# Conditioning groups of a 1-core model kernel closed one by one, and its tiles placed anew over the layers

## The reference

```python
def first_block(x, ...):            # DEPTH = 2: attention, then mLSTM
    h = x
    for i in range(DEPTH):
        if i % 2 == 0: h = h + dilated_attention_mixer(rms_norm(h, attn_norm[i // 2]), ...)
        else:          h = h + mlstm_mixer(rms_norm(h, mlstm_norm[i // 2]), ...)
        h = h + swiglu(rms_norm(h, ffn_norm[i]), ffn_w_in[i], ffn_w_out[i])
    return rms_norm(h, final_norm)

def second_block(x, c, ctx, ...):   # layers: neighbourhood attention, conformer, short conv, neighbourhood attention
    for i in range(4):
        mod_l = (silu(c) @ mod_w[i] + mod_b[i]).reshape(b, 6, 1, 1024)
        mod_c = (silu(c_ctx) @ mod_w[i] + mod_b[i]).reshape(1, 6, 1, 1024)
        a = rmsnorm(x, norm1_g[i]) * (1 + mod_l[:, 1]) + mod_l[:, 0]
        x = x + mod_l[:, 2] * mixer_i(a, ...)
        m = rmsnorm(x, norm2_g[i]) * (1 + mod_l[:, 4]) + mod_l[:, 3]
        x = x + mod_l[:, 5] * (square(relu(m @ mlp_w1[i])) @ mlp_w2[i])
        # the same for ctx with mod_c, while a later attention still needs it
    return rmsnorm(x, final_g)
```

## Time and profile before

| | |
|---|---|
| time, median of 3 runs | 3109.58 us (3107.96 to 3117.44) |
| the profiled execution's own time | 3106.95 us |
| its span in the profile | 3104.8 us |
| PE busy | 2923.8 us |
| DVE busy | 2011.8 us |
| ACT busy | 1186.5 us |
| POOL busy | 357.5 us |
| DMA | 451.79 MB, mean 146 GB/s |

### The profile page before, as it was taken

One profiled execution on the slowest core, in us unless ns is written; L12 is line 12 of the kernel. 1 busy time (PEld: TensorE's weight loads), 2 busy tenths in 40 slices (PEclk: granted clock), 3 DMA queues, 4 the chain that ended last, 5 costly groups with the idle time before them and its releaser, 6 DMA issues.

```text
span 3104.8 us, 41474 instructions
## 1 busy us (share of the span) xinstructions
PE 2923.8 (94%) x17130; PEld 2499.0 (80%) x17130; DVE 2011.8 (65%) x3228; ACT 1186.5 (38%) x1927; POOL 357.5 (12%) x539
## 2 busy tenths in 40 slices
PE   7998999889989989999999899999999999998898
PEld 7998899879977767888865578887877888777898
DVE  6776777767765667666653576666767664444665
ACT  5443443544443443332231442223224222343544
POOL 0000101000013221000123100001010000143000
PEclk9999999989989999999999999999999999999999
DMA  6544566436646543444445334443443442366353
GB/s 223 166 167 143 171 230 225 138 125 227 232 156 136 106 72 103 151 142 150 147 135 149 104 129 142 154 145 128 143 143 122 148 151 95 85 106 95 123 182 131
DMA packets 362269, 451.79 MB, mean 146 GB/s; under 512 B 12656, under 2 KB 332432, under 8 KB 362080
## 3 DMA queue, kind: packets, MB, share of 16 engines
q1 hardware_dynamic: 326976, 329.89, 32.5%
q0 software_dynamic: 34944, 118.65, 15.2%
q10 hardware_dynamic: 160, 0.59, 0.1%
HBM read 438.67 MB, written 1.05 MB: 142 GB/s over the span
## 4 chain that ended last, share of the span: by engine, by line
PE 79%; DVE 11%; ACT 5%; issue 3%; DMA 2%; POOL 1%; SPq 0%; DVEq 0%; ACTq 0%; POOLq 0%
PE ps L1025 23%; PE ps L1027 23%; PE ps L1026 23%; DVE MX L1551 2%; DVE lo L1497 2%; PE ps L1194 2%; DVE lo L1500 2%; ACT hi L1226 1%; PE ps L1181 1%; PE ps L1046 1%; PE ps L1048 1%; PE ps L1047 1%; DMA NB<-in_na_rpb 1%; PE ps L1090 1%; DVE NB L1509 1%
## 5 line engine op out<-in xcount | busy, mean ns | idle before, releaser
L1025 PE MATMUL ps<-XN,hi 128*128 128x256 f32 (+1 forms) x3008 | 1023.2, 340 | 79.0 <-DVE XN L1523 31.8
L1026 PE MATMUL ps<-XN,hi 128*128 128x256 f32 (+1 forms) x3008 | 1009.4, 336 | 0.0
L1027 PE MATMUL ps<-XN,lo 128*128 128x256 f32 (+1 forms) x3008 | 1008.4, 335 | 0.0
L1025 PEld LDWEIGHTS ps<-XN,hi 128*128 128x128 f32 x3008 | 584.9, 194 | 165.0 <-DVE XN L1523 39.1
L1027 PEld LDWEIGHTS ps<-XN,lo 128*128 128x128 f32 x3008 | 584.6, 194 | 54.8
L1026 PEld LDWEIGHTS ps<-XN,hi 128*128 128x128 f32 x3008 | 585.4, 195 | 52.8
L1497 DVE TENSOR_TENSOR lo<-raw,hi 128x1024 fp32r<-128x1024 f32 (+1 forms) x313 | 385.3, 1231 | 290.1 <-ACT hi L1226 287.8
L1551 DVE CUSTOM_DVE_ANT_0 MX<-MW,C 128x1024 bf16<-128x1024 f32 x384 | 485.5, 1264 | 40.4 <-DMA MW<-in_mod_w 33.8
L1226 ACT ACTIVATE hi<-raw 128x1024 fp32r<-128x1024 f32 (+1 forms) x313 | 326.2, 1042 | 439.9 <-PE ps L1027 436.0
L1500 DVE TENSOR_TENSOR lo<-raw,hi 128x1024 fp32r<-128x1024 f32 (+1 forms) x313 | 381.6, 1219 | 0.0
L1027 PE MATMUL ps<-H,lo 128*128 128x512 f32 (+1 forms) x1024 | 371.2, 363 | 0.0
(11 more groups left out here) (225 smaller groups left out, 3417.4 us busy)
## 6 DMA issues: line engine op xcount, KB each, us to landing
raw<-in_mlp_w SPq DMA_DIRECT2D x128, 1024.0 KB, 5.0
MW<-in_mod_w POOLq DMA_DIRECT2D x192, 512.0 KB, 3.8
raw<-in_ffn_w_in SPq DMA_DIRECT2D x44, 1024.0 KB, 5.0
raw<-in_attn_w_in SPq DMA_DIRECT2D x36, 1024.0 KB, 4.9
raw<-in_na_wqkv SPq DMA_DIRECT2D x24, 1024.0 KB, 4.9
raw<-in_ffn_w_out SPq DMA_DIRECT2D x16, 1024.0 KB, 5.0
raw<-in_mlstm_w_in SPq DMA_DIRECT2D x12, 1024.0 KB, 5.0
raw<-in_cv_w SPq DMA_DIRECT2D x12, 1024.0 KB, 6.3
```

What stands on the lines that cost most here:

```text
L1025: e.matmul(out, whi, xhi, start=first, stop=False)
L1026: e.matmul(out, whi, xlo, start=False, stop=False)
L1027: i = e.matmul(out, wlo, xhi, start=False, stop=last)
```

## The change

- A layer's groups close one by one: `mod_close` runs after tiles 15, 23, 39 and 47 of a layer, each over its own groups; `("mod", layer, group)` and `("gs", layer, which)` are separate names, and each norm and residual waits for its own. `conditions_for(layer, group)` asks for the tiles up to that group only, and now stands before residuals too.
- `beside` adds half the pace, and is called after each tile of a unit, not in the first unit after a norm (`outer`) and not in the last unit before one (`quiet`).
- Paces: none in attention and mLSTM, 0.65 in SwiGLU, 0.25 in neighbourhood attention, 1.15 from the first MLP to the third, 0.5 in the last MLP.
- The loads of C and of the first MW stand after the first unit of attention instead of ahead of all.

```diff
@@ -246,6 +246,9 @@
 
+CLOSING = {15: (0, 2, 0), 23: (2, 3, None), 39: (3, 5, 1), 47: (5, 6, None)}
+
+
@@ -332,17 +335,17 @@
             self.do("mod_load", n + 1)
-        if n % 48 == 47:
-            self.do("mod_close", n // 48)
+        if n % 48 in CLOSING:
+            self.do("mod_close", n // 48, *CLOSING[n % 48])
 
     def beside(self):
-        self.credit = min(self.credit + self.pace, 2.0)
+        self.credit = min(self.credit + self.pace / 2, 2.0)
         if self.credit >= 1:
...
 
-    def conditions_for(self, layer):
-        while self.parts < (layer + 1) * 48:
+    def conditions_for(self, layer, i):
+        while self.parts < layer * 48 + (i + 1) * 8:
             self.condition()
@@ -350,7 +353,7 @@
 
-    def linear(self, w, layer, k0, kt, c0, cols, x, evac, adv=1, outer=False, until=None):
+    def linear(self, w, layer, k0, kt, c0, cols, x, evac, adv=1, outer=False, until=None, quiet=False):
 
@@ -370,7 +373,7 @@
                 evac(t, *banks[i])
-            if group[-1] == tiles[-1] // 2 or outer:
+            if not (outer or quiet):
                 self.beside()
@@ -387,7 +390,7 @@
             evac(t, b, u)
-            if t == ntt // 2 - 1:
+            if t % (ntt // 2) == ntt // 2 - 1:
                 self.beside()
@@ -422,7 +425,7 @@
         if shift is not None:
-            self.conditions_for(shift[0])
+            self.conditions_for(shift[0], shift[1] + 1)
         s = self.rstd(n)
@@ -436,6 +439,8 @@
     def residual(self, j, n, gate, b, u, last):
+        if gate is not None:
+            self.conditions_for(*gate)
         self.do("residual", self.norms, j, n, gate, b, u, last)
@@ -455,7 +460,7 @@
             self.linear(w, layer, 0, KT, c * 256, 256, x, evac, adv=adv if first else 1, outer=bool(first),
-                        until=first)
+                        until=first, quiet=c == 3)
             if first:
@@ -483,6 +488,10 @@
 
+    def begin_conditions():
+        p.do("conditions")
+        p.do("mod_load", 0)
+
@@ -495,7 +504,7 @@
                 if first:
-                    p.pend.append(lambda: p.do("conditions"))
+                    p.pend.append(begin_conditions)
                 p.pend.append(rotate)
@@ -534,7 +543,7 @@
                     p.do("product", j, t, k, kt, banks[t], ("hf", layer, k0), kk == 0, kk == 21)
-                if t == 0:
+                if c < 3:
                     p.beside()
@@ -804,7 +813,7 @@
 
-        p.linear("cv_w2_2", 0, 0, KT, c * 256, 256, ("cn", 0, 0, 512), evac, outer=c == 0)
+        p.linear("cv_w2_2", 0, 0, KT, c * 256, 256, ("cn", 0, 0, 512), evac, outer=c == 0, quiet=c == 3)
 
@@ -847,7 +856,7 @@
 
-            p.linear("mlp_w2_2", layer, q * D, KT, c * 256, 256, ("h2", layer, q, n), evac)
+            p.linear("mlp_w2_2", layer, q * D, KT, c * 256, 256, ("h2", layer, q, n), evac, quiet=q == 3 and c == 3)
 
@@ -859,30 +868,31 @@
     p.do("begin")
-    p.do("mod_load", 0)
     for j in range(KT):
...
     p.do("tables", LNEXP)
-    p.pace = 0.4
     attention(p)
-    p.pace = 0.6
+    p.pace = 0.65
     swiglu(p, 0)
-    p.pace = 0.4
+    p.pace = 0.0
     mlstm(p)
-    p.pace = 0.6
+    p.pace = 0.65
     swiglu(p, 1)
     between(p)
-    p.pace = 1.0
+    p.pace = 0.25
     neighbourhood(p, 0, 0, True)
+    p.pace = 1.15
     mlp(p, 0, 512)
...
     mlp(p, 2, 512)
+    p.pace = 0.25
     neighbourhood(p, 3, 1, False)
+    p.pace = 0.5
     mlp(p, 3, S)
@@ -982,10 +992,11 @@
         e.dma_start(m.PV[:, :, :], T["params"]).then_inc(*sig["pv"].says("params"))
+        e.dma_start(m.pos[:, :], T["positions"].broadcast_to([32, S])).then_inc(*sig["pos"].says("positions"))
+
+    def conditions():
         for s in range(2):
             e.dma_start(m.C[:, s, :], T["cond"][s:s + 1, :].broadcast_to([P, D])).then_inc(*sig["cond"].says("cond"))
-        e.dma_start(m.pos[:, :], T["positions"].broadcast_to([32, S])).then_inc(*sig["pos"].says("positions"))
-
@@ -1007,7 +1018,7 @@
 
-    go_through(p, {"begin": begin, "load": load, "cv_spread_one": cv_spread_one, "finish": finish})
+    go_through(p, {"begin": begin, "load": load, "conditions": conditions, "cv_spread_one": cv_spread_one, "finish": finish})
 
@@ -1247,7 +1258,7 @@
             return
-        w.wait_ge(("mod", shift[0]))
+        w.wait_ge(("mod", *shift), ("gs", *gain[1:]))
         for i in range(n // S):
@@ -1537,7 +1548,7 @@
             return
-        w.wait_ge(("mod", gate[0]))
+        w.wait_ge(("mod", *gate))
         for i in range(n // S):
@@ -1552,20 +1563,21 @@
 
-    def mod_close(layer):
-        i, r = layer * 48 + 47, ROW["mod_b_2"] + 6 * layer
+    def mod_close(layer, i0, i1, which):
+        r = ROW["mod_b_2"] + 6 * layer
         mods = m.mod[:, layer, :, :].rearrange("p (i k) s -> p i k s", i=6)
-        w.wait_ge(("mod_part", i, 1), "params")
+        w.wait_ge(("mod_part", layer * 48 + i1 * KT - 1, 1), "params")
         for s in range(2):
-            e.tensor_tensor(mods[:, :, :, s], mods[:, :, :, s],
-                            m.PV[:, :, r:r + 6].rearrange("p k i -> p i k"), ALU.add).then_inc(
-                *dve.says(("biased", layer)))
-        w.wait_ge(("biased", layer))
-        for which, name in ((0, "norm1_g_2"), (1, "norm2_g_2")):
-            i, r = 1 + 3 * which, ROW[name] + layer
-            e.scalar_tensor_tensor(out=m.gs[:, layer, which, :, :], in0=m.mod[:, layer, i * KT:(i + 1) * KT, :],
-                                   scalar=1.0, in1=m.PV[:, :, r:r + 1].broadcast_to([P, KT, 2]), op0=ALU.add,
-                                   op1=ALU.mult).then_inc(*dve.says(("mod", layer)))
+            e.tensor_tensor(mods[:, i0:i1, :, s], mods[:, i0:i1, :, s],
+                            m.PV[:, :, r + i0:r + i1].rearrange("p k i -> p i k"), ALU.add).then_inc(
+                *dve.says(("biased", layer, i0), *[("mod", layer, i) for i in range(i0, i1)]))
+        if which is None:
+            return
+        w.wait_ge(("biased", layer, i0))
+        r = ROW[("norm1_g_2", "norm2_g_2")[which]] + layer
+        e.scalar_tensor_tensor(out=m.gs[:, layer, which, :, :], in0=m.mod[:, layer, (i0 + 1) * KT:i1 * KT, :],
+                               scalar=1.0, in1=m.PV[:, :, r:r + 1].broadcast_to([P, KT, 2]), op0=ALU.add,
+                               op1=ALU.mult).then_inc(*dve.says(("gs", layer, which)))
 
...
         A = m.ang
```

## The result

| | before | after |
|---|---|---|
| median | 3110.74 us (4 runs, 3107.96 to 3117.44) | 3135.25 us (4 runs, 3132.90 to 3137.84) |
| profiled execution, its span | 3106.95, 3104.8 us | 3133.35, 3131.5 us |
| ratio, 95% interval | | 1.0076 (1.0057 to 1.0095) |

The change makes the kernel 24.5 us slower. The forecast was 3152, with a range of 3122 to 3178; the sign and the mechanism came as predicted, the size is 17 us under the forecast. In spans, the two profiled executions differ by 26.7 us. The ratios in this document leave out two single executions that took far longer for a reason unknown, 5735 us in experiment 5 and 15530 us in experiment 8; the medians there are taken with them.

What follows compares the result with a forecast made beforehand. TensorE, busy in 94% of the span, was taken as the bound, with about 181 us idle. Costs 80.0 less gains 37.2 give +42.8 us on 3106.95: 3149.8, or 3152.4 for the median; range 3122 to 3178.

Steps and rivals of the forecast that it cites:

- The count of tiles: The credit counter, counted in the code: eight tiles missing at the last MLP's norm, five more at its first down product.
- Cost 1: Last MLP's norm: eight demanded tiles run in a row, and TensorE has nothing for 47.3 us.
- Cost 2: Last MLP's first down product: five demanded tiles in a row, and TensorE stands still for 25.3 us.
- Rival B: Demands dearer: reloads at 7.8 instead of 6.6 us, second neighbourhood's tiles on the path; 3170 us, chance 0.12.
- The closing: Two additions and one scaled product after the demanded tiles in the last MLP, taken at 0.8 us.
- Clock after the stalls: Last MLP: the second stall adds 3.4 us of slow clock; twice as long would add 3.4 for each.
- First neighbourhood: First neighbourhood attention: gain 10 us, from 5.6 behind bias-table loads and three tiles' part of PT-copy waits, 1.5 each.
- attention: Attention: gain 7.2 us, three of 16 tiles standing directly before a copy or residual; bounds 2.4 and 32.7.
- rival A: The moved work wins in the early stages, each tile worth 2.4 us: 20 us faster, about 3090; chance 0.06.
- clock term: Gain of 6.8 us (0 to 10), stage not named, from two slow clock stretches of 3.4 us less.
- Rival C: Second demand in the last MLP covered, or gains half as large again: 25 us less, 3127; chance 0.10.
- D: Tiles spread to the end as announced, no burst, the counter being wrong: 37 less 4, 3076; chance 0.02.

Runs made afterwards that it cites:

- experiment 5: The kernel before with only the loads of C and the first MW moved behind the first unit of attention: 3109.01 us, ratio 0.9992.
- experiment 8: The changed kernel with pace 0.83 instead of 0.65 in both SwiGLUs and 1.2 in the MLPs: 3093.36 us, ratio 0.9931.
- experiment 1: The changed kernel with pace 1.3 instead of 1.15 from the first MLP to the third: 3058.71 us, ratio 0.9823.
- experiment 4: The kernel before with pace 0.0 instead of 0.4 in attention and 0.75 instead of 0.6 in the SwiGLUs: 3115.39 us, ratio 1.0015.
- experiment 7: experiment 1 with the closing by groups undone, so each norm and residual demands a whole layer: 3137.79 us, ratio 1.0082.

## Why the prediction was right, and where its sizes were off

**The count of tiles** was right to the tile: TensorE stalls where eight and where five were missing, and with all sixteen placed earlier by experiment 1 neither stall is there.

**Cost 1**, 47.3 us: measured 47.0 (49.81 less the 2.77 of before). **Cost 2**, 25.3: measured 27.19. Two steps were off. The reload of its first waiting tile took 5.42 us of wait instead of 4.1, while 240 GB/s flowed against 131 beside the later ones; the shorter closing gave 0.4 of that back. And the units that cover the stall lasted 5.4 us from the first tile's start (2961.01 to 2966.38) instead of 6.6. Rival B's objection, that no weight load is in flight in a stall, did not hold for this one tile.

**The closing**, taken at 0.8 with bounds of 0 and 1.65: 0.6 us (2900.23 to 2900.83).

**Clock after the stalls**, 3.4: an estimate of 2 from the second stall (half of the 4 us that TensorE works at the lower level), and at the first less than before the change. The granted clock in four stretches, the first of before and three of after (columns as in rows 2):

```profile
2908.60:2914.20 5.60, 5.60 (x26) 5.60 (x27) 5.19 (x13) 4.18 (x8) 0.00 (x0) 0.50 0.00 0
...
2903.00:2906.00 3.00, 3.00 (x17) 3.00 (x17) 3.00 (x9) 1.97 (x4) 0.00 (x0) 0.57 0.11 44
2906.00:2910.00 4.00, 4.00 (x36) 4.00 (x35) 3.59 (x7) 2.79 (x4) 0.00 (x0) 1.00 0.00 0
...
2994.00:2998.00 4.00, 4.00 (x22) 4.00 (x22) 3.61 (x5) 0.00 (x0) 0.00 (x0) 0.54 0.56 169
```

After the stall of 50 us TensorE works at the 1.2 GHz level for 3 us only, and after the 27 us stall for 4. Before the change, 5.6 us of the 7 in the earlier trace rows are work, after a gap of 2.77 us; the first 1.2 us of the slow stretch pass while TensorE still waits, so its price was nearer 2.8 than the 3.4 of the prediction. The upper bound "twice as long" was on the wrong side. That activity releases the slow state, as the Trainium skill, "TensorE: Matmul & The Clock Gate", section "What's actually happening", says, agrees with the trace: one slow stretch for a stall, which ends 3 and 4 us after TensorE has work again.

**Three tiles in the second neighbourhood**, 3 (0 to 7.5): 0.0. **The demanded tile at the second MLP's norm**, 1: 0.0. **Forgotten**: the three tiles spread in the last MLP's up products, which I had as hidden. They cost 0.75, 1.61 and 1.62 us of TensorE, 4 in all. The sum of costs, predicted 80.0, is 79.8 by the stretch of the last MLP; that this is so close is luck, since the missing 4 and the 2 too few of cost 2 stand against three small terms that were too high.

**Gains**, predicted 37.2, measured 53. Start 4: 3.1. mLSTM 7.2: 8.7. First neighbourhood 10: 10.5, but not as it was added up: the 5.6 us behind the tables' loads are gone as predicted, the waits for PT copies fell by 1.3 only (10.3 to 9.0) instead of 4.5, and 3.7 us are busy time at a higher granted clock, 0.98 instead of 0.96; that the sum came out is luck. The term that was mis-sized is **attention**, 7.2 and its share of the clock: it gave 21.3. The busy times of the stage after the change (columns as in rows 2):

```profile
17.00:317.00 300.00, 280.05 (x2188) 273.61 (x2188) 199.71 (x340) 138.01 (x233) 4.41 (x6) 0.98 0.45 150
```

Idle TensorE time falls from 32.7 to 19.95, 12.7 us, and busy time from 287.3 to 280.05, 7.3 us, with the granted clock up from 0.94 to 0.98. The step that failed is "three of the 16 tiles stand directly before a copy". The first mix (the product of PT and V) of before and of after, in TensorE's timelines:

```profile
107.99 2.29 PE L1090 MATMUL ps<-PT,V 128*128 128x256 f32 x7 [5.19 <-DVE PT L1636]
```

```profile
100.41 2.23 PE L1101 MATMUL ps<-PT,V 128*128 128x256 f32 x12 [2.47 <-DVE PT L1648]
```

No tile stands directly ahead of this copy, and yet its wait halves. The waits of 5.19, 5.76 and 7.14 us before the first mixes of three pairs are 2.47 or 2.48 now, one value; that is 10.7 of the 12.7 us of idle time, and TensorE's waits for this copy over the span fall from 21.7 us to 11.1. Before the change, the last tiles ahead of the three copies started 22.2, 12.3 and 2.4 us before them, so only the third stood directly ahead. That tiles also counted from far ahead is shown: experiment 4 takes them away, and their loads with them, with nothing else changed up to the stage's end, and the stage takes 300.0. How the delay is carried is argued and not shown. I take it to be a backlog on VectorE, but between the first of those tiles and its copy VectorE is idle for 4.1 us, 3.4 of it waiting for ScalarE's work on PB, so the delay goes through both engines. The predicted rival A had this mechanism with its bound, 2.4 a tile; measured are 1.33, its share of the clock included, so the moved work wins only where the demands do not stand against it. The two slow stretches of the clock term, 6.8, came to more than twice that: TensorE's whole busy time is 15.9 us shorter with the same 17130 matmuls, 7.3 of it in the attention.

Rival B (dearer demands) is contradicted by the 6.6 us between GpSimd's issues in the stall. Rival C had two mechanisms: the second demand covered, which is not so (27.2 us), and gains half as large again, which is nearly what happened; its time, 3127, lies 8 us under the measured one, the forecast 17 over. So the forecast was right in its costs, and the 16 us by which it missed in spans (42.8 predicted, 26.7 measured) are the gains that were too small. (Its chance of faster, A and D, adds up to 0.08 and not 0.07.)

## What to carry to other kernels

When background work is metered by a counter, run the counter on paper to every point that demands it: one pace 13% too low cost 80 us, nearly four times the 21.3 us that the best of the early stages gained. A demand in a row costs the round trip of its buffer, here 6.6 us for 2.5 us of work, so spread tiles further apart than a round trip, or give the demand a second buffer. Price the extra work on a queue by the whole stage, not by the instructions directly ahead of a wait.

## What the runs showed of the hardware

After a long stall the granted clock comes back once, a few us after TensorE has work again, and how many does not go by the length of the stall. At the 1.2 GHz level TensorE worked for 3.0 us after the stall of 49.81 us and for 4.1 us after the one of 27.19 us; for 5.7 and 3.3 us in experiment 7, after 51.19 and 36.77 us; and for 5.6 us before the change, after a gap of 2.77 us. In the long stall the rest of the slow stretch passes while nothing runs and costs nothing (granted 0.52 from 2852.8 to 2903):

```profile
2852.80:2903.00 50.20, 0.40 (x2) 0.43 (x3) 21.07 (x39) 2.26 (x6) 4.28 (x8) 0.52 0.27 93
```

So the time at the lower level is no measure of what it costs. From before to after it grows by 5 us in all (194 to 199), but the part of it in which TensorE works falls from 142 to 105 us, and with it TensorE's busy time falls by 15.9 us.
